# A hybrid decoder layer on one core: output projection two tiles behind, next x turned first, gates on ScalarE, blocks written out

## The reference

```python
mod = silu(c) @ w_ada + b_ada            # six vectors: sh1, sc1, gt1, sh2, sc2, gt2
h   = rms_norm(x, g_pre_mix) * (1 + sc1) + sh1
cv, cg, q, f, i, g = split(h @ w_in)     # six groups of 512 columns
# convolution group
u = cv * sigmoid(cg)
u = causal depthwise conv(u, width 31) + dw_bias
y_conv = silu(layer_norm(u, conv_ln_gain, conv_ln_bias))
# recurrent group: 4 heads of 128, chunks of 64 tokens
qf, forget = silu(q), lb + (1 - lb) * sigmoid(f)
k, b = 1 - forget, cumsum(log(forget)) in the chunk
q_dec, k_inv, k_end = qf * exp(b), k * exp(-b), k * exp(b_last - b)
o = causal(q_dec k_inv^T) i + q_dec state      # state: carried over the chunks
y_rec = rms_norm(o, rec_norm_gain) * silu(g)
x1 = x + gt1 * rms_norm(concat(y_conv, y_rec) @ w_out, g_post_mix)
h2 = rms_norm(x1, g_pre_ffn) * (1 + sc2) + sh2  # routing logits, then the experts
out = x1 + gt2 * rms_norm(hier_moe(h2), g_post_ffn)
```

## Time and profile before

| | |
|---|---|
| median of 3 runs | 1842.06 us (1839.32 to 1843.01) |
| profiled execution | 1839.05 us, span 1837.5 us |
| instructions | 24383 |
| TensorE busy | 1533.9 us, 83% |
| VectorE busy | 1296.4 us, 71% |
| ScalarE busy | 841.1 us, 46% |
| GpSimd busy | 374.0 us, 20% |
| mean granted TensorE clock | 0.914 |

### The profile page before, as it was taken

One profiled execution on the slowest core, in us unless ns is written; L12 is line 12 of the kernel. 1 busy time (PEld: TensorE's weight loads), 2 busy tenths in 40 slices (PEclk: granted clock), 3 DMA queues, 4 the chain that ended last, 5 costly groups with the idle time before them and its releaser, 6 DMA issues. The chain is left out here.

```text
span 1837.5 us, 24383 instructions
## 1 busy us (share of the span) xinstructions
PE 1533.9 (83%) x7268; PEld 1152.0 (63%) x7270; DVE 1296.4 (71%) x1999; ACT 841.1 (46%) x1443; POOL 374.0 (20%) x403
## 2 busy tenths in 40 slices
PE   2597945699998899998899998926989999999960
PEld 2486824488855789666689475425667666666730
DVE  5489966679965499865599652257667877778738
ACT  1422232433363522454322542313767787878745
POOL 1000000000010000010000010114546666665640
PEclk9999966799998899998899998956989999999985
DMA  9255114133322232322331122372999998889948
GB/s 341 76 157 187 52 43 163 64 94 107 98 81 71 81 110 73 92 92 92 84 100 47 38 89 81 126 237 82 314 338 301 302 341 263 241 229 315 279 97 363
DMA packets 200424, 291.29 MB, mean 159 GB/s; under 512 B 10558, under 2 KB 158171, under 8 KB 200346
## 3 DMA queue, kind: packets, MB, share of 16 engines
q1 hardware_dynamic: 169762, 193.03, 31.4%
q0 software_dynamic: 30416, 97.19, 18.9%
q10 hardware_dynamic: 168, 0.06, 0.0%
HBM read 240.42 MB, written 59.26 MB: 163 GB/s over the span
## 5 line engine op out<-in xcount | busy, mean ns | idle before, releaser
L892 DVE SCALAR_TENSOR_TENSOR cv<-u,taps,cv 128x512 f32<-128x512 f32 x480 | 321.7, 743 | 0.6 <-DVE yT L848 0.3
L1741 DVE TENSOR_TENSOR w_rest<-wgu,w_high 128x1024 fp32r<-128x1024 f32 x192 | 233.7, 1221 | 94.5 <-ACT w_high L1666 93.3
L1666 ACT ACTIVATE w_high<-wgu 128x1024 fp32r x192 | 201.5, 1054 | 139.3 <-PE pgu L1616 86.0
L416 PE MATMUL bank<-hT_high,tiles_operand 128*128 128x512 f32 x512 | 204.6, 400 | 35.7 <-DVE hT_operand L866 21.1
L417 PE MATMUL bank<-hT_operand,tiles_operand 128*128 128x512 f32 x512 | 203.2, 397 | 0.0
L418 PE MATMUL bank<-hT_high,win_operand 128*128 128x512 f32 x512 | 202.9, 396 | 0.0
L439 PE MATMUL bank<-wo,yT 128*128 128x512 f32 x432 | 189.7, 594 | 0.0
L1626 PE MATMUL py<-wd,hTe 128*128 x384 | 172.6, 592 | 0.9 <-ACT yb L1693 0.9
L1614 PE MATMUL pgu<-w_high,x_high 128*128 128x512 f32 x384 | 155.3, 404 | 0.0
L1616 PE MATMUL pgu<-w_high,x_rest 128*128 128x512 f32 x384 | 151.0, 393 | 0.0
L1615 PE MATMUL pgu<-w_rest,x_high 128*128 128x512 f32 x384 | 151.0, 393 | 0.0
(11 more groups left out here) (345 smaller groups left out, 2910.4 us busy)
## 6 DMA issues: line engine op xcount, KB each, us to landing
win<-w_in_in SPq DMA_DIRECT2D x64, 512.0 KB, 5.2
wgu<-w_gate_in SPq DMA_DIRECT2D x32, 1024.0 KB
wgu<-w_up_in SPq DMA_DIRECT2D x32, 1024.0 KB
wd<-w_down_in SPq DMA_DIRECT2D x32, 1024.0 KB
wo<-w_ada_in POOLq DMA_DIRECT2D x8, 2048.0 KB, 9.2
win<-w_in_in SPq DMA_DIRECT2D x16, 1024.0 KB, 5.2
y_dram<-zeros POOLq DMA_DIRECT2D x17, 512.0 KB, 5.3
win<-x_in SPq DMA_DIRECT2D x16, 512.0 KB, 4.5
```

The source lines that it names most:

```text
L416: nc.tensor.matmul(out[:], high[:, k, cols], hT_high[:, k, :], start=(k == 0), stop=False)
L892: ins = V.scalar_tensor_tensor(out=cv[:, j], in0=u[:, j, w:w + T], scalar=tap, in1=cv[:, j], op0=ALU.mult, op1=ALU.add)
L1666: A(w_high[:, QK * q:QK * q + QK, :], c.wgu[:, bass.ds(slot, 1), QK * q:QK * q + QK, :].rearrange("p a k n -> p (a k) n"), ACT.Copy).then_ ...
L1741: V.tensor_tensor(w_rest[:, part, :], c.wgu[:, bass.ds(slot, 1), part, :].rearrange("p a k n -> p (a k) n"), w_high[:, part, :].bitcast(F3 ...
```

## The change

- **Output projection two tiles behind.** The `y`, `r`, `l` steps of stage t are now for tiles 4t - 2 to 4t + 1, not 4t - 4 to 4t - 1: the last two of the block before and the first two of this block. Block 0's stage so has four half tiles, and the tail two tiles. `yT` holds two tiles. The gate over the outputs, its transposes and the copies into `yT` go tile by tile.
- **Next x turned first.** `T` and what follows it stand at the head of the stage. `project` of blocks 1 to 3 starts with unit 2; units 0 and 1 (piece 0) are in the list, as `piece`. `win_high` has three slots, shared with `yt` and `xres`.
- **Gates on ScalarE.** The forget gate and 1 - forget are `Identity` activations with scale and bias; the output gate is a Silu from PSUM into a buffer `gs` of its own; the convolution's swish is one Silu in place of a Sigmoid and two VectorE operations.
- **Modulation.** Parts 7, 8 and 9 are done on TensorE, by one-column matmuls from the loaded weights (`ada_part`), not on VectorE; vector 5 stays there.
- **Blocks written out.** The hardware loops are gone, and the order of SP's loads is pieces 0 and 1, then x.

```diff
-        STEPS = [("y", 0, 0), ("mean",), ("y", 0, 1), ("y", 1, 0), ("var",), ("A", 0), ("y", 1, 1), ("B", 0), ("r", 0), ("O", 0),
...
+        tile_no = lambda t, w: t * NT - 2 + w
...
+            ORDER = [("y", 0, 0), ("ada", 0), ("T", 0), ("T", 1), ("mean",), ("T", 2), ("ada", 1), ("y", 0, 1), ("T", 3), ("var",),
...
+            def ada_part(out, p, j, first, final):
+                for k in range(4):
+                    last = nc.tensor.matmul(out[:, j:j + 1], ada_slot[slot_of(p)][:, k, j * P:(j + 1) * P],
+                                            cond[:, 4 * (p % 2) + k:4 * (p % 2) + k + 1], start=first and k == 0,
+                                            stop=final and k == 3, skip_group_check=True)
+            def project(t):
+                for n in range(2 if t > 0 else 0, AU):
+                    piece_half(t, n)
+                    if t == 0 and n in (15, 17):
+                        ada_columns(2 if n == 15 else 3)
...
 # state_sums, outputs, turn_outputs
+                if i >= 2:
+                    pe.wait_ge(yT_rec, t * NT + i - 1)
-                                                c.state[:, (2 * i + s) % 4, cols_of(h)], start=False, stop=(s == 1 and h == NH - 1),
+                                                c.state[:, s, cols_of(h)], start=False, stop=(s == 1 and h == NH - 1),
-                if i == 0:
-                    pe.wait_ge(o_gated, t + 1)
+                pe.wait_ge(o_gated, t * NT + i + 1)
...
 # ScalarE, split_piece
+                if j == 1 and t > 0:
+                    act.wait_ge(logit_ready, tile_no(t - 1, 3) + 1)
 # ScalarE, gates
+                for h in range(NH):
+                    n = t * NH + h
+                    act.wait_ge(q_parts, 3 * n + 3)
+                    A(ki[:, h], ki[:, h], ACT.Identity, scale=c.oneless[:, h:h + 1], bias=c.lb[:, h:h + 1]).then_inc(forget_ready, 1)
+                    act.wait_ge(forget_ready, n + 1)
+                    act.wait_ge(q_gated, n + 1)
+                    A(ke[:, h], ki[:, h], ACT.Identity, scale=-1.0, bias=c.ones[:, 0:1]).then_inc(ke_ready, 1)
-                        A(ob[:, 2 * half:2 * half + 2, cols], src, ACT.Copy).then_inc(g_parts, 1)
-                act.wait_ge(g_parts, (t + 1) * 4)
-                act.wait_ge(conv_step, (t + 1) * CONV_STEPS)
-                A(gs, ob[:], ACT.Silu).then_inc(g_done, 1)
+                        A(gs[:, 2 * half:2 * half + 2, j * 256:(j + 1) * 256], src, ACT.Silu).then_inc(g_parts, 1)
 # ScalarE, conv_gate
-                    A(hT[:, k, :], cv[:, k], ACT.Sigmoid, scale=col("conv_ln_gain", k), bias=col("conv_ln_bias", k)).then_inc(ln_sig, 1)
+                    A(cv[:, k], cv[:, k], ACT.Silu, scale=col("conv_ln_gain", k), bias=col("conv_ln_bias", k)).then_inc(ln_out, 1)
...
 # VectorE, head_gates
-                    V.tensor_scalar(ki[:, h], ki[:, h], c.oneless[:, h:h + 1], c.lb[:, h:h + 1], ALU.mult, ALU.add).then_inc(forget_ready, 1)
-                    ch.step(V.tensor_tensor(qd[:, h], qd[:, h], ke[:, h], ALU.mult))
-                    ch.step(V.tensor_scalar(ke[:, h], ki[:, h], -1.0, 1.0, ALU.mult, ALU.add))
+                    V.tensor_tensor(qd[:, h], qd[:, h], ke[:, h], ALU.mult).then_inc(q_gated, 1)
 # VectorE, gate_outputs, now for one tile
-                V.tensor_tensor(o3, o3, sums[:, 32:48].unsqueeze(2).to_broadcast([P, NT * NH, P]), ALU.mult).then_inc(v_rec, 1)
-                V.tensor_tensor(ob[:], ob[:], gs[:], ALU.mult).then_inc(o_gated, 1)
+                    last = V.scalar_tensor_tensor(out=ob[:, i % 2, hc], in0=ob[:, i % 2, hc], scalar=sums[:, 32 + 4 * i + h:33 + 4 * i + h],
+                                                  in1=gs[:, i, hc], op0=ALU.mult, op1=ALU.mult)
 # SP
-                for i in range(2):
-                    load_x(t, i)
-                for j in range(2):
-                    load_piece(t, j)
+                    for j in range(2):
+                        load_piece(t, j)
+                    for i in range(NT):
+                        load_x(t, i)
```

More of the change, by code:

```diff
@@ L373, in _, with take, turn_in @@
         def _(pe):
-            def ring(units, before, banks=bank):
-                size = len(banks)
-                for n in range(len(units)):
-                    if n >= size:
-                        wait(pe, *reader(*units[n - size]))
-                    elif before and n >= size - 4:
-                        wait(pe, *reader(*before[n - size + 4]))
-                    yield banks[n % size]
-            def turn_in(t, i, banks):
+            taken = {}
+            def take(kind, i, half, t):
+                n = bank_of((kind, i, half), t)
+                if n in taken:
+                    pe.wait_ge(*taken[n])
+                taken[n] = reader((kind, i, half), t)
+                return bank[n]
+            def turn_in(t, i):
                 pe.wait_ge(x_normed, t * NT + i + 1)
                 for half in range(2):
-                    out = next(banks)
+                    out = take("T", i, half, t - 1)
                     for j in range(4):
@@ L432, in y_half @@
-            def y_half(t, i, half, banks):
-                if i == 0 and half == 0:
+                    last = nc.tensor.matmul(out[:, j:j + 1], ada_acc[m][:, j * P:(j + 1) * P],
+                                            c.ones[:, 0:1], start=True, stop=m != 3, skip_group_check=True)
+                    if m == 3:
+                        last = ada_part(out, 7, j, False, True)
+                if m == 3:
+                    last.then_inc(ada_used, 1)
+                    pe.wait_ge(ada_used, 1)
+                    pe.sem_inc(ada_cols_done, 1)
+                else:
+                    last.then_inc(ada_cols_done, 1)
@@ new lines, in ada_half @@
+            def ada_half(half):
+                p = 8 + half
+                if half == 0:
+                    for n in range(2):
+                        pe.wait_ge(*taken[n])
+                pe.wait_ge(*ada_load(p))
+                for j in range(KD):
+                    last = ada_part(bank[1][:, 0:KD], p, j, half == 0 and j == 0, half == 1)
+                last.then_inc(ada_used, 1)
+                if half == 1:
+                    pe.wait_ge(ada_used, 3)
+                    pe.sem_inc(ada_cols_done, 1)
@@ L445, in router_turn @@
                 for half in range(2):
-                    out = next(banks)
+                    out = take("r", i, half, t)
                     for j in range(4):
@@ L450, in router_turn, with logits @@
                     last.then_inc(rT_ready, 1)
-            def logits(t, i, banks):
-                pe.wait_ge(rin_ready, t * 2 * NT + 2 * i + 2)
-                out = next(banks)
+            def logits(t, i):
+                pe.wait_ge(rin_ready, 2 * tile_no(t, i) + 2)
+                out = take("l", i, 0, t)
                 for k in range(KD):
@@ new lines, in steps @@
+            def steps(t):
+                for kind, *at in ORDER:
+                    if not present(kind, at, t):
+                        continue
+                    if kind in NEXT_WORK:
+                        {"xsum": x_sums, "raw": raw_input, "high": high_input, "split": split_piece}[kind](t + 1, *at)
+                    else:
+                        {"ln": log_forget, "exps": head_exps, "end": end_exp, "sq": squares, "var": variance, "gate": conv_gate,
+                         "ysum": y_sums, "x1sum": x1_sums, "rin": router_in, "key": save_keys, "osq": square_outputs,
```

771 lines of the change are left out of this document (364 added, 407 removed), and 9 rows, old and new, of tables (ORDER, STEPS).

## The result

The kernel after takes 1770.35 us (median of 4, 1766.94 to 1780.75) against 1841.95 for the kernel before on the same chip (1839.32 to 1843.01): ratio 0.9623, 95% interval 0.9588 to 0.9658, so 71.6 us less. The forecast was 1771. It came out right partly because two errors cancelled.

The account below looks back on a forecast made before the run. It took TensorE to bound the projections, with waits in four mixing stages and the tail. Gains 5.9 + 2 x 11.8 + 9.1 + 32.2 = 70.8 took 1839.05 to 1768.3, median forecast 1771, range 1745 to 1808.

Parts of the forecast that it names:

- Block 0: First projection and mixing stage 0: projection ends at 225.1, first two units end near 362 against 367.85, a gain of 5.9 us.
- TensorE does it in 32 one-column matmuls: First projection: the fourth modulation's second half on TensorE costs 7.4 us less what it did there; a 4.37 us stall goes.
- a mixing stage 0 past 365: Block 0: sign that the forecast is wrong, if mixing stage 0 runs past 365 us; its first two units were put near 362.
- Blocks 1 and 2: Middle blocks: a period of 250.9 us instead of 262.7, a gain of 11.8 in each.
- the slow spell: Mixing stages of blocks 1 and 2: 3.0 us added for slow matmuls after the 4.2 us idle at turn 1.
- The 1 us for the rest of piece 10: Projections: gates on ScalarE delay this weight piece's split, costing 0 to 3 us a block, taken as 1.
- Block 3 and the tail: Last block and output tiles: gains of 9.1 us in block 3 and 32.2 in the tail, 75.3 to 43.1.
- Unrolling: Loops over blocks written out: a taken branch costs 0.03 us, so no gain or loss.
- B: Rival, mixing stages and tail: full overlap, TensorE never waits in the new stages; 106 us gained, 1736; chance 0.10.
- C: Rival, mixing stages: the ScalarE and VectorE chain keeps every stage's length, only the tail shortens; 1810; chance 0.10.
- E: Rival, block 0: output weights load late, and if VectorE is 15 us later the first stage loses that; 1786; chance 0.11.
- D: Rival, mixing stages: waits pull TensorE's clock to the lower level, 6.95 us more per half, 16 halves give 1882; chance 0.06.

Follow-up runs that it names:

- e1: The kernel after with the fourth modulation's second half summed on VectorE again, 8 one-column matmuls instead of 40: 1759.79 us, ratio 0.9557.
- e4: The kernel after with the forget gate and one minus it computed on VectorE again instead of ScalarE: 1769.28 us, ratio 0.9609.
- e8: The kernel before with its five loops over blocks written out and nothing else changed: 1848.58 us, ratio 1.0050.
- e11: The kernel after, unchanged, run and profiled a second time: 1769.15 us, ratio 0.9603.
- e5: The kernel after with the next block's x turned late again, at the stage's end, output projection still two tiles behind: 1825.75 us, ratio 0.9918.
- e3: The kernel after with the fourth modulation's 40 one-column matmuls cut into four lots of 10 behind successive projection units: 1766.82 us, ratio 0.9592.

## Why the prediction came out right

Against the first profile (own time 1780.75, forecast for it 1768.3, 12.5 over):

- **Block 0: wrong, 12.8 us.** The step that failed is "TensorE does it in 32 one-column matmuls, four times the 1.84 of the earlier trace rows, 7.4 us, less what it did there". It has two faults. The 8 column sums are still there, so that nothing was to be taken off: 40 matmuls are five times 1.84, 9.2 us, where 7.4 stood for all of them. And the upper level was assumed: the stretch took 15.0 us (12.5 to 15.3 in the seven profiles), 5.8 over the 9.2. Projection 0 ended at 235.5 (232.7 again) and not 225.1, and these two make 7.6 of the 10.4. Of the rest 1.65 is a wait ahead of unit 14, 2.19 us at 159.31 for 0.54 in before, which had the third modulation's columns (1.84 us) just ahead of that wait and now has them behind unit 15; 0.7 came earlier and 0.4 are slow units. That e1 ends its projection at 225.2 is chance: it has neither the stretch nor the saved stall. In the stage the two halves cost 11.7 and 12.8, inside the bounds of 7.4 to 14.3; scores 0 waited 6.3 us for the head decays, outputs 0 began at 296.9, which is the 286 foreseen plus the 10. The other 2.4 are in this stage. Predicted y(1) 484.2 (362 and 122.2), measured 497.0 and 491.2. The first two units end near 374.8, so the prediction's own sign of being wrong, a mixing stage 0 past 365, did come.
- **Blocks 1 and 2: right, 3.3 us a block too dear.** Turn 1 waits 3.66 (4.2), scores 0 at m 44.3 (43.7), y(2,0) at m 69.5 (67.9), logits 3 end at m 119.9 (119.2, or 122.2 with the slow spell that I had added). The slow spell is there (turn 1 1.94 us, the mean's rows 5.39 against 3.60 elsewhere), yet the 22 last units begin at m 125.5, 0.8 past the 124.7 of the walk without it, so 3.0 for it was too much; what other part of the walk was priced too high by as much is not shown. The 1 us for the rest of piece 10 is nothing: TensorE has no wait in these projections, and e4 prices the gates within 1 us a block.
- **Block 3 and the tail: right.** 110.3 for 111.0 (the 110.0 and the 1.0 of its projection); 44.4 for 43.1, as the tail's four halves take 30.3 and not 27.8 (the granted clock is 0.85) and the last chain 14.1 and not 15.3.
- **Unrolling: wrong as a term, without effect on the sum.** By e8 it costs the kernel before 7.9 us. In the kernel after the output gate is taken out of the banks by Silu within the projection, and its table load (at 476.56) stands in ScalarE's idle time, so the cost is not in it. I had looked at TensorE's idle at the branch only, not at what writing out moves on ScalarE.
- **The untouched phase** added 5.2 in that one execution.

So the errors are 12.8 - 6.8 - 0.7 + 1.3 + 5.2 = 11.8 of 12.5. The last 0.7 lie outside the stages' span. In e11, an execution near the median, they are 7.0 (block 0), -6.6, 0.6 (block 3 with tail 154.7 for 154.1) and -0.5 (the untouched phase): 0.5, and it took 1769.05 for 1768.3. The right total rests on a block 0 priced too low and two blocks priced too high.

The rivals: B, full overlap, did not come; TensorE keeps 7 us of idle a stage. C, the chain stays, is what e5 builds: 1825.8, where C gave 1810. E did not come: block 0's first output half waits 0.71 us, and for VectorE, not for a load. D's clock is 0.93 to 0.95 in stages 1 to 3, above its bound of 0.85; but D named the right resource in the wrong place, the clock is the largest part of what block 0 lost. The Trainium skill, "TensorE: Matmul & The Clock Gate", section "Why this matters for your kernels", ties drops of the clock to idle gaps between bursts; the one-column stretch has no such gap (14.7 of 15.0 us busy) and drops all the same, so here the measurement decides.

## What to carry to other kernels

When work goes to an engine that is the bound just then, price it at the lower clock if its instructions are short: one-column matmuls took the clock down with no idle at all, and the matmuls behind them paid too. Two edits that are argued together should be parted by one kernel that has only one of them (e5): here early x is the gain of every period, two tiles behind that of the end, part of which block 0 pays back. Before writing a loop out, look at what each engine holds ahead of a wait, a table load above all. And before a few us are read out of one profile, see how far the same code spreads over the others: projection 0 of the kernel after ended 3.8 us apart, which hides all that e3 gained.

## What I had not expected of the hardware

- A stretch of 40 one-column matmuls halves the granted clock (1.00 ahead of it, 0.50 at its end; 8 records 1.03 us, then 1.85) while TensorE is recorded busy, in all seven profiles that have it.
- Cut into lots of 10, each lot runs at the upper level, and behind three of the four the spell falls on the work that follows (0.59, 0.76 and 0.55 just behind them; 1.00 behind the third).
- Writing out a loop moved a 1.28 us table load behind a wait in each of two blocks, and the kernel took 7.9 us longer; with the load asked for early it did not.
- A phase with the same code takes 623.9 to 632.3 us over the profiles of all kernels, and 631.8 and 626.1 in two executions of one.
